# Product-key experts: U and V rows gathered and used pair by pair instead of all U rows, then all V rows

## The reference, cut to what matters

```
q = (xt @ wq).reshape(t, 8, 2, 128)
sc = einsum('thkd,hknd->thkn', q, keys)
s1, i1 = top_k(sc[:, :, 0], 16);  s2, i2 = top_k(sc[:, :, 1], 16)
cand = (s1[..., :, None] + s2[..., None, :]).reshape(t, 8, 256)
top_s, ci = top_k(cand, 16)
experts = i1[ci // 16] * 128 + i2[ci % 16]      # t x 8 x 16
gates = softmax(top_s)
ub = u_tab[experts]
act = gelu(einsum('td,thkd->thk', xb, ub)) * gates
vb = v_tab[experts]
y = einsum('thk,thkd->td', act, vb)
```

## Time and profile before

| | us |
|---|---|
| median of 3 runs | 3589.15 |
| lowest and highest | 3585.93, 3603.69 |
| the profiled execution, its own time | 3594.65 |
| its span, first to last instruction | 3592.8 |

### The profile page before, as it was taken

The page is one execution under the profiler, slowest core; times in us unless marked ns, Lnnn a source line. Parts: engine busy times, 40 slices in busy tenths (PEclk is TensorE's granted clock), DMA queues, the critical chain, the costliest instruction groups (busy, mean ns, idle before and its releaser), DMA issues.

```text
span 3592.8 us, 43362 instructions
## 1 busy us (share of the span) xinstructions
PE 2642.7 (74%) x17252; PEld 2247.3 (63%) x17252; DVE 1715.0 (48%) x3881; ACT 1281.2 (36%) x1784; POOL 1618.7 (45%) x1389
## 2 busy tenths in 40 slices
PE   5521788228950686228868988888999999889999
PEld 3421577117830575116647877776999998778887
DVE  5599827884688836880026244554210113531010
ACT  2100476017720475018733322333332322533131
POOL 0045555666566655666612222222454633136463
PEclk7665899659975898659979978998999999999999
DMA  5198899999999999999912100000233322013332
GB/s 183 63 342 316 309 334 381 376 357 322 388 381 349 345 358 391 392 373 348 340 43 63 50 1 1 1 1 18 65 90 87 94 83 59 13 48 95 99 94 77
DMA packets 360653, 694.21 MB, mean 193 GB/s; under 512 B 35784, under 2 KB 215155, under 8 KB 360323
## 3 DMA queue, kind: packets, MB, share of 16 engines
q0 software_dynamic: 147456, 536.94, 40.1%
q1 hardware_dynamic: 212995, 154.50, 13.6%
HBM read 689.26 MB, written 2.10 MB: 192 GB/s over the span
## 4 chain that ended last, share of the span: by engine, by line
PE 54%; DVE 17%; issue 8%; DMA 7%; ACT 6%; another core or an unknown queue 5%; POOL 2%; SPq 0%; ACTq 0%; DVEq 0%
PE PS L1669 27%; PE PS L827 6%; DMA ring<-in_peer_v,eidx 6%; DVE ring L1389 6%; ACT ring L1025 3%; PE PS L707 2%; PE PS L878 2%; PE PS L1570 2%; POOL ring L655 1%; PE PS L1579 1%; PE PS L808 1%; PE PS L1576 1%; PE PS L1691 1%; DVE acc L2481 1%
## 5 line engine op out<-in xcount | busy, mean ns | idle before, releaser
L655 POOL DMA_INDIRECT ring<-in_peer_u,eidx x512 | 483.1, 943 | 493.9 <-DVE act_d L1389 199.7
L1669 PE MATMUL PS<-held_uH,GW 128*128 128x264 f32 (+1 forms) x3008 | 661.9, 315 | 20.1 <-POOL BIG_value L2206 16.0
L827 PE MATMUL PS<-C,ring 128*128 128x128 f32 x4096 | 543.7, 282 | 169.4 <-ACT ring L1025 90.2
L1025 ACT ACTIVATE ring<-ring,gact 128x1024 f32<-128x1024 f32 x512 | 576.3, 1147 | 222.7 <-DMA ring<-in_peer_v,eidx 168.5
L655 POOL DMA_INDIRECT ring<-in_peer_v,eidx x512 | 493.6, 964 | 328.1 <-PE PS L827 234.1
L1389 DVE CUSTOM_DVE_ANT_0 ring<-ring,PS 128x1024 f32<-128x1024 f32 x512 | 606.6, 1217 | 55.3 <-DMA ring<-in_peer_u,eidx 30.5
L2192 POOL TENSOR_TENSOR GW<-held_wr,GW 128x1024 fp32r<-128x1024 f32 x178 | 429.0, 2412 | 435.4 <-ACT GW L1961 435.4
L827 PEld LDWEIGHTS PS<-C,ring 128*128 128x128 f32 x4096 | 464.7, 144 | 245.4 <-ACT ring L1025 125.9
L1669 PEld LDWEIGHTS PS<-held_uH,GW 128*128 128x128 f32 x3008 | 503.0, 193 | 62.2 <-issue 17.1
L1669 PE MATMUL PS<-BIG_value,GW 128*128 128x264 f32 (+1 forms) x1504 | 447.2, 313 | 0.0
L1669 PE MATMUL PS<-hid,GW 128*128 128x264 f32 (+1 forms) x2304 | 366.5, 321 | 0.0
(11 more groups left out here) (465 smaller groups left out, 3480.8 us busy)
## 6 DMA issues: line engine op xcount, KB each, us to landing
held_wr<-in_w_ff SPq DMA_DIRECT2D x128, 512.0 KB, 4.0
wqr<-in_peer_wq SPq DMA_DIRECT2D x64, 512.0 KB
held_wr<-in_w_in_ab SPq DMA_DIRECT2D x18, 512.0 KB, 3.8
ring<-in_peer_u,eidx POOLq DMA_INDIRECT x512
ring<-in_peer_v,eidx POOLq DMA_INDIRECT x512
BIG<-in_w_in SPq DMA_DIRECT2D x4, 1536.0 KB, 11.6
held_wr<-in_w_qkv_c SPq DMA_DIRECT2D x12, 512.0 KB, 3.9
w_out<-in_w_out SPq DMA_DIRECT2D x1, 4096.0 KB, 19.9
```

The lines of the kernel that those rows point to most:

```text
L655: e.indirect_dma_start(out=ring[:, i % RING, :], out_offset=None, in_=rows_u if k < HK else rows_v, in_offset=bass.IndirectOffsetOnAxis(ap ...
L827: ins = e.matmul(bank[6 + j // 4][:, j % 4 * P:(j % 4 + 1) * P], row[:, j * P:(j + 1) * P], ident, start=(k == 0 and j % 4 == 0), stop=(k ...
L1025: e.mul(row, row, gact[:, k:k + 1]).then_inc(*n.up(e_scaled))
L1669: ins = e.matmul(bank[b + a][:, 0:w], (hi, lo)[w_][:, k * P:(k + 1) * P], (x_hi, x_lo)[x_][:, c0:c0 + w], start=(first and w_ == 0 and x_ ...
```

## The change

Expert k of a block is now a pair. The ring has five slots of 2048 floats. POOL waits once per pair, for the transposes of pair i - 5, and issues the U gather into the first half and the V gather into the second half; both add to one semaphore. DVE takes the dot, ACT takes gelu of the one column, its product with the gate, and the scaling of the V row; PE transposes and adds up. The list has for each k one u and one v entry, with front steps between pairs.

What goes with it:
- The heads run ahead: at the end of block b the front of block b + 1 has four heads done (AHEAD = 4), and the other four run among the first pairs. Front steps are 150 and spread evenly over the 128 pairs. In block 3 the remaining 28 steps stand among the first 32 pairs, and the tails of blocks 0 to 2 behind pair 56.
- The gates come in batches of heads: (0,1), (1,2), (2,4), (4,8) in block 0, and (0,4), (4,8) in the others.
- `hn` is made by eight transposes on PE from `hnT`, after the last dot of the block before; the weights of that norm are applied by DVE when it takes `hnT` out of PSUM. `gffn` and its load are gone.
- S5 uses one pair of banks instead of two; its output uses bank 0; the sums are turned back through banks 0 and 1.
- The second slot of the query weights is now `W4[:, 3, :]` (for the very first, a row of the ring); the first such load of a block waits on SP until `hs` has been transposed.
- Constants used only at the start are loaded apart into the ring.

The diff, cut to its core:

```diff
-RING = 7
+RING = 5
+AHEAD = 4
+BATCHES = [[(0, 1), (1, 2), (2, 4), (4, 8)]] + [[(0, AHEAD), (AHEAD, 8)] for blk in range(1, NB)]
-FIRST_PART = 112
+FRONT_ENDS, SECOND_AT = 32, 56
...
+    def experts(blk, others, total):
+        done = 0
         for k in range(HK):
...
+            weigh()
             order.append(("u", blk, k))
+            if k == HK - 1 and blk < NB - 1:
+                order.append(("hn", blk + 1))
+            if k == 1 and blk:
+                order.append(("done", blk - 1))
+            shares()
+            order.append(("v", blk, k))
...
+            upto = total(k + 1)
+            while done < upto:
+                step(others)
+                done += 1
...
     def first_pool(e):
         for blk in range(NB):
+            for k in range(HK):
+                i = HK * blk + k
+                if k % TOPK == 0:
                     e.wait_ge(r_idx, NH * blk + k // TOPK + 1)
+                if i >= RING:
+                    e.wait_ge(e_pv, i - RING + 1)
+                for a in range(2):
+                    e.indirect_dma_start(
+                        out=ring[:, i % RING, D * a:D * a + D], out_offset=None, in_=tables[a],
+                        in_offset=bass.IndirectOffsetOnAxis(ap=eidx[:, blk % 2, k:k + 1], axis=0),
+                    ).then_inc(d_r[i % RING], 16)
+    def pair_there(i):
+        return d_r[i % RING], 32 * (i // RING + 1)
...
+            if blk and m == 1:
+                e.wait_ge(r_hTp, 2 * blk + 2)
+            e.dma_start(query_slot(i), wqv[m]).then_inc(d_q[i % NQ], 16)
...
+    def turn_normed(e, n, blk):
+        e.wait_ge(r_hT, 2 * blk + 2)
+        if blk:
+            e.wait_ge(e_dot, HK * blk)
+        for k in range(8):
+            ins = e.transpose(hn[:, k * P:(k + 1) * P], hnT[:, k, :], ident)
+        ins.then_inc(*n.up(e_hn))
...
+    def weigh_row(e, n, blk, k):
+        i = HK * blk + k
+        a, row = act[:, k:k + 1], ring[:, i % RING, D:2 * D]
+        e.wait_ge(e_dot, i + 1)
+        e.activation(a, a, ACT.Gelu).then_inc(*n.up(e_gelu))
+        if k % TOPK == 0:
+            e.wait_ge(r_gate, batches_to(blk, k // TOPK))
+        e.wait_ge(e_gelu, i + 1)
+        e.mul(a, a, gate[:, blk % 2, k:k + 1]).then_inc(*n.up(e_gact))
+        e.wait_ge(e_gact, i + 1)
+        e.mul(row, row, a).then_inc(*n.up(e_scaled))
...
     def keep_sums(e, n, blk):
+        if blk < NB - 1:
+            e.wait_ge(r_idx, NH * (blk + 1) + AHEAD)
...
-        e.scalar_tensor_tensor(hs, Xb, sm[:, 5:6], gffn[:, :], ALU.mult, ALU.mult).then_inc(*up(r_hs))
+        e.tensor_scalar(hs, Xb, sm[:, 5:6], None, ALU.mult).then_inc(*up(r_hs))
+        yield from s.to(HT + 1)
+        for half in range(2):
+            e.wait_ge(*nxt(r_hTp))
+            e.tensor_tensor(hnT[:, 4 * half:4 * half + 4, :], f4(bank[half]), vp(76 + 4 * half, 4), ALU.mult).then_inc(*up(r_hT))
```

More of the change, by code:

```diff
@@ L86, in constants @@
     two["ident"] = one["ident"]
-    two["ones"] = one["ones"]
-    return one, two
+    two["ones"] = np.ones((P, P), f)
+    return one, once, two
 def pack(parts):
@@ L176, in heads @@
         return (taken.get(("front", blk), 0) - Q_AT - 6) // Q_ROWS
[L178 to L189, removed]
-        for k in range(HK):
-            while heads(blk) < min(NH, (k + 8) // TOPK + 1):
+    batches = [(blk, h0, h1) for blk in range(NB) for h0, h1 in BATCHES[blk]]
@@ new lines, in first_order, with weigh, shares @@
+    weighed = []
+    def weigh():
+        while batches and heads(batches[0][0]) >= batches[0][2]:
+            batch = batches.pop(0)
+            order.extend([("shift",) + batch, ("power",) + batch])
+            weighed.append(("share",) + batch)
+    def shares():
+        order.extend(weighed)
+        del weighed[:]
+    def experts(blk, others, total):
+        done = 0
+        for k in range(HK):
+            need = (k + 8) // TOPK + 1
+            for h0, h1 in BATCHES[blk]:
+                if TOPK * h0 <= k + 4:
+                    need = max(need, h1)
+            while heads(blk) < min(NH, need):
@@ L207, in experts @@
+            if k == 1 and blk:
+                order.append(("done", blk - 1))
+            shares()
+            order.append(("v", blk, k))
+            if blk == NB - 1 and k == SECOND_AT:
+                order.append(("second",))
+                others += [(("tail", b), TAIL_STEPS) for b in range(3)] + [(("pproj", 3), 2)]
+            upto = total(k + 1)
+            while done < upto:
+                step(others)
+                done += 1
+            weigh()
         order.append(("end", blk))
@@ L684, in setup_tensor @@
             e.wait_ge(s_bt, 1 + a)
-            turn(e, bank[6 + a], ring[:, 5, 512 * a:512 * a + 512]).then_inc(*n.up(s_tp))
+            turn(e, bank[6 + a], rows[:, 5, 512 * a:512 * a + 512]).then_inc(*n.up(s_tp))
             yield
@@ L1002, in front_scalar @@
         square_mean(e, n, hs, Xb, sm[:, 5:6], sm[:, 4:5], D)
-        yield from s.to(HT + 1)
-        for half in range(2):
-            e.wait_ge(r_hTp, 2 * blk + 1 + half)
-            e.copy(W4[:, 0, 512 * half:512 * half + 512], bank[half]).then_inc(*n.up(r_hT))
-        yield from s.to(Q_AT + 2)
-        if blk:
-            e.wait_ge(e_dot, HK * blk)
-        e.copy(hn, hs).then_inc(*n.up(e_hn))
         for h in range(NH):
```

267 lines of the change are left out of this document (124 added, 143 removed).

## The result

| | us |
|---|---|
| before, median of 4 runs | 3587.54 (3581.4 to 3603.69) |
| after, median of 4 runs | 3690.39 (3681.26 to 3692.13) |
| ratio | 1.0274, 95% interval 1.0237 to 1.0312 |
| span of the profiled execution after | 3679.5 |

What follows compares the result with a forecast made beforehand. The prediction took the gather stretch, paced by the ring's slots, as the bound: 604.5 + 271.5 + 699 us of pairs plus 10 gave 1585 against 1635, so 3539 us, 8 in 10 between 3410 and 3680.

Steps and rivals of the forecast that it cites:

- What bounds the kernel: Gather stretch: 1635 us for 1024 gathers, no engine full; the 1958 us of the span outside it stay unchanged.
- The cycle's terms: One pair from first gather to freed slot: gathers, landing, dot, gelu, product, scaling, transposes, handovers; 11.8 us without waiting.
- Waiting: Pair's in-order queues: 2.15 us as in the last V stage plus 1.0 for DVE; cycle 14.95 us, 3.0 per pair.
- Rest: 237 pairs at 2.95: Pairs beside neither heads nor S5, taken as having only light steps: 2.95 us each, 699 us together.
- DVE stretches: Pairs beside DVE's heavy front steps: 186 with heads at 3.25 us, 89 with S5 at 3.05 us.
- Tables: ACT in the gather stretch: some 80 table loads against 34, 59 us more, hidden inside the waiting.
- The smaller edits: Norm weights on DVE, dot operand by PE, weight slots, gate batches, constants: nothing or a few us each.
- The second, in-order coupling: Rival: engines' in-order queues hold pairs and their slots; pace 3.4 us per pair, plus 116 us, 3705; chance 0.27.
- a pace of 2.8: Gather stretch, between the DMA-limited rival and the forecast: 3460 us; DMA-limited or near 2.8 had chance 0.15.
- one of 2.7: Gather stretch, us per pair: the fast end of the 8-in-10 range, given as 3410 us.
- 2.95 to 3.12: Gather stretch, average us per pair: the forecast's own range, given as 3500 to 3570 us, chance 0.42.

Runs made afterwards that it cites:

- no_gelu: The changed kernel with a plain copy in place of each pair's gelu: 3669.91 us, ratio 1.0243 to the kernel before.
- grouped_r7: All of the change but the pairs: 128 U rows, then 128 V rows, ring of 7 rows of 4 KB: 3543.4 us, ratio 1.0021 to the kernel before.
- rows55: The changed kernel with 5 U and 5 V rows, each freed by its own last reader: 3670.6 us, ratio 1.0223 to the kernel before.
- lag1: rows55 with each V row one pair behind its U row, in list and gathers: 3490.9 us, ratio 0.9878 to the kernel before.
- grouped_r10: grouped_r7 with a ring of 10 rows of 4 KB instead of 7: 3481.14 us, ratio 0.9844 to the kernel before.

## Why the prediction was wrong

**What bounds the kernel** held: all of the loss lies in the gather stretch, and 1955 us outside it answer to the 1958.

**The cycle's terms** held, but for one. Gelu and product take 0.20 and 0.295 us (0.25 each), the dot 1.21, scaling 1.15. Landings in the chain of block 1 take 5.61 to 7.17 us (6.1). That speaks once more against the estimate of 3.2 us that the Trainium skill's formula (DMA: Bandwidth & Descriptors, "Anatomy of one DMA — SWDGE (gpsimd) path") gives for them. The transposes did not hold: 8 x 736.8 / 4096 = 1.44 us instead of 1.1. The granted clock was 0.77 and not the 0.97 of a V stage, and the 8 transposes of a pair take between 0.87 us (724 to 748 us) and 1.97 us (992 us).

**Waiting** is the step that failed. I added 1.0 us for DVE's queue to a V stage's 2.15, as if the queues were independent. With the terms now measured, 1.25 + 6.1 + 1.21 + 0.5 + 1.15 + 1.44 + 0.5 make 12.2 us; the cycle seen is 5 x 3.34 = 16.7. Waiting was 4.5 us instead of 3.15. Its cause is the chain DVE, ACT, PE, DVE, in which each front step that PE or DVE does first holds the same pair once more. The lag showed that: same steps, same rows, and 3.4% less with one pair of lag, 2.7% (101 us) with four beside an equally fast kernel before.

**"Rest: 237 pairs at 2.95"** is where most of it stands. I priced DVE's steps and the query weights, and took all other steps as light. But they hold the projection, 22 us of PE per block in the chain above, and the first output projection, 9 us, which U rows had covered; the second one stood beside V rows before too. The 16 pairs of block 1 from the 32nd on took 72 us, 4.5 each. A part of the term was wrong even without other steps: I took 2.95 from the 24 pairs of block 3 that have none, and they ran at 3.66 beside the loads for later parts. I asked of each new place of a step what DVE does there, and never what PE does.

**DVE stretches**: S5 ran at 2.9 us per pair where I had 3.05. Heads ran at 3.1 to 3.5 where I had 3.25. Both were near.

**Tables**: 80 loads in the stretch, as forecast, 1.28 us each. That they lie inside other waiting held (no_gelu, 0.3%).

**The smaller edits** held: grouped_r7 is at 1.0021.

**The rivals.** The second, in-order coupling with 5.2 us of waiting, is what happened: it gave 3705, the median is 3690. Of its reasons DVE's wait for scores and PE's projection were seen; the slot whose U row lies idle (rows55, 0.5%) and the table loads (no_gelu, 0.3%) were not the cause, so that its number came so near is in part luck. I gave it 0.27, since V stages today run heads and transposes side by side. That was no evidence. In a V stage the weights of the rows are known long before, ACT's waits are mostly for landings, and the loop through a dot does not exist.

**Slips in the sum.** By my own sum a pace of 2.8 gives 3398 and not 3460, one of 2.7 gives 3346 and not 3410, and 2.95 to 3.12 give 3474 to 3561 and not 3500 to 3570. The lower end of the range belonged to a pace of 2.82. None of it bears on the outcome, which lies on the other side.

## What to carry to other kernels

When two passes become one, list for every engine what it now waits for within one item, and see whether the list closes to a loop through in-order queues; if it does, put one item of lag between the producer's and the consumer's entries. Price every step at its new place on every engine, above all the one that was idle beside it before. And split a change: here the SBUF that was freed was worth 1.8% in the old order, and the new order cost 3.9%.

## What was not expected of the hardware

The mean granted clock of PE over the gather stretch hardly changed: 0.79 before (the stages of the earlier trace rows, weighted with their lengths) and 0.76 after. What changed is where PE's work stands. Before, the transposes ran in V stages at 0.93 to 0.98, and the 0.60 to 0.63 of the U stages fell on little work. Now they are spread over the whole stretch, and the same 4096 transposes took 736.8 us instead of 543.7. Such a mean is time at both of its levels, 0.5 and 1.0, mixed; evening out PE's load made its busy time longer.

How little of that comes through to the time can be read from two other runs (lines over the stretch, lag1, then grouped_r10):

```profile
L883 PE MATMUL PS<-C,ring 128*128 128x128 f32 x4096 | 682.3, 324 | 449.9 <-ACT ring L1079 448.6
```
```profile
L879 PE MATMUL PS<-C,ring 128*128 128x128 f32 x4096 | 521.1, 278 | 116.8 <-ACT ring L1068 115.6
```

161 us more of busy PE, at clocks of 0.82 and 0.80 from 171 to 1700 us, and yet the ratios are only 0.3% apart (0.9878 and 0.9844, beside kernels before of 3532 and 3534 us). There most of it lies inside PE's waiting. In the changed kernel, where PE stands in a closed loop of waits, its share was not measured by itself.
